# Weight slots as contiguous rows, cast once, and read back in bf16 from a scratch tensor

## The reference

```
h = rmsnorm(x); [u | gb | gc | v] = h @ w_in              # 1024 -> 2048
A = (trailing means of u over 2/4/8/16 tokens - u) @ w_pool * scale
B = gb * causal_conv3(gc * v)
x += [A | B] @ w_out                                      # 1024 -> 1024
h = rmsnorm(x); up = causal_conv3(h @ w_up) + bias        # 1024 -> 2 x 2816
x += (silu(gate) * val) @ w_down                          # 2816 -> 1024
y = rmsnorm(x)                                            # and new pool, conv and ffn states
```

## Time and profile before

| | us |
|---|---|
| median of 3 runs | 893.31 |
| lowest and highest run | 893.15, 897.61 |
| span of the profiled execution (slowest core, core 5) | 899.7 |
| the other cores' spans | 853.4 to 892.1 |
| PE busy | 743.1 (83%) |
| DVE, ACT, POOL busy | 506.7, 360.7, 345.8 |

### The profile page before, as it was taken

The page is one execution under the profiler, slowest core; times in us unless marked ns, Lnnn a source line. Parts: engine busy times, 40 slices in busy tenths (PEclk is TensorE's granted clock), DMA queues, the critical chain, the costliest instruction groups (busy, mean ns, idle before and its releaser), DMA issues.

```text
span 899.7 us, 13434 instructions; the slowest of 8 cores (853.4 to 899.7 us)
## 1 busy us (share of the span) xinstructions
PE 743.1 (83%) x3826; PEld 336.7 (37%) x3826; DVE 506.7 (56%) x878; ACT 360.7 (40%) x846; POOL 345.8 (38%) x501
## 2 busy tenths in 40 slices
PE   1765797698999669977899869988899778988996
PEld 0322353344454324433344324433344334333442
DVE  2463467578744635666654646666643645766832
ACT  3221355466722222554552223554542322645621
POOL 5342037477610320466640320566630320566500
PEclk9979899799999989999999979999999989999999
DMA  8999469999972893599992695699992792899921
GB/s 237 140 133 141 65 63 138 133 108 111 86 94 83 175 139 38 51 115 122 123 108 94 171 154 49 56 122 117 125 98 94 158 143 29 74 112 120 118 83 71
DMA packets 265451, 98.74 MB, mean 110 GB/s; under 512 B 251662, under 2 KB 256142, under 8 KB 265378
## 3 DMA queue, kind: packets, MB, share of 16 engines
q0 software_dynamic: 257280, 70.93, 85.0%
q1 hardware_dynamic: 8098, 26.95, 9.2%
HBM read 158.75 MB, written 10.01 MB: 188 GB/s over the span
## 4 chain that ended last, share of the span: by engine, by line
PE 42%; DMA 36%; DVE 8%; issue 7%; ACT 6%; POOL 1%; SPq 1%; DVEq 0%; ACTq 0%; POOLq 0%
PE G L450 24%; DMA wslot<-w_up 21%; DMA wslot<-w_in 11%; PE G L665 8%; PE G L664 8%; ACT hbuf L391 2%; DMA xrot<-xp 2%; DMA x<-xp 2%; DVE x L672 1%; DVE x L673 1%; PE TR L414 1%; PE G L690 1%; ACT rs_all L393 1%; DVE hbuf L403 1%; ACT hb L391 1%
## 5 line engine op out<-in xcount | busy, mean ns | idle before, releaser
L450 PE MATMUL G<-aT,wslot 128*128 128x512 bf16 x1408 | 324.3, 385 | 36.8 <-DMA wslot<-w_up 29.7
L373 POOL DMA_DIRECT2D wslot<-w_up x176 | 158.6, 903 | 168.5 <-PE G L450 122.2
L450 PEld LDWEIGHTS G<-aT,wslot 128*128 128x128 bf16 x1408 | 133.5, 99 | 218.1 <-issue 76.6
L774 ACT ACTIVATE arena<-G,cst_sb 128x512 f32<-128x512 f32 x176 | 134.8, 777 | 146.1 <-PE G L450 146.0
L783 DVE SCALAR_TENSOR_TENSOR arena<-G,cst_sb,arena 128x512 f32<-128x512 f32 x176 | 130.4, 750 | 101.6 <-ACT Esave L799 71.5
L450 PE MATMUL G<-hT,wslot 128*128 128x512 bf16 x512 | 129.3, 411 | 57.2 <-DMA wslot<-w_in 48.7
L803 POOL TENSOR_TENSOR actT<-arena 128x512 bf16<-128x512 f32 x88 | 95.9, 1090 | 114.1 <-ACT arena L770 76.0
L664 PE MATMUL G<-w_down_sb,actT 128*128 128x512 bf16 x352 | 133.4, 379 | 0.0
L665 PE MATMUL G<-w_down_sb,actT 128*128 128x512 bf16 x352 | 133.4, 379 | 0.0
L792 DVE SCALAR_TENSOR_TENSOR arena<-G,cst_sb,arena 128x512 f32<-128x512 f32 x176 | 125.5, 745 | 5.0 <-DVE OFp L790 0.5
L373 POOL DMA_DIRECT2D wslot<-w_in x64 | 57.5, 902 | 139.5 <-PE G L450 138.4
(11 more groups left out here) (116 smaller groups left out, 612.2 us busy)
## 6 DMA issues: line engine op xcount, KB each, us to landing
wslot<-w_up POOLq DMA_DIRECT2D x176, 256.0 KB, 10.7
wslot<-w_in POOLq DMA_DIRECT2D x64, 256.0 KB, 18.9
x<-xp SPq DMA_DIRECT2D x16, 512.0 KB, 12.2
yp<-x SPq DMA_DIRECT2D x16, 512.0 KB, 2.9
xrot<-xp SPq DMA_DIRECT2D x12, 512.0 KB, 8.1
w_down_sb<-w_down POOLq DMA_DIRECT2D x11, 512.0 KB, 20.5
w_out_sb<-w_out POOLq DMA_DIRECT2D x4, 512.0 KB, 31.1
stf_sb<-st_ffn SPq DMA_DIRECT2D x1, 704.0 KB, 8.0
```

The costliest lines, as they stand in the source:

```text
L373: P.op("pool", lambda e, slot=slot, c0=c0, src=src: e.dma_start(out=wslot[slot][:, :, c0:c0 + 128], in_=src.rearrange("(k p) n -> p k n", ...
L450: ins = e.matmul(out_ap, lhsT=wslot[slot][:, k, half * 128:(half + 1) * 128], rhs=rhsT[:, k, 0:ncols], start=(k == 0), stop=(k == nk - 1))
L774: P.op("act", lambda e, tp=tp, g=g, c=c, h=h: e.activation(out=tp[:, h, 2:514], in_=G[g][:, :], func=AF.Identity, scale=cc(C_FW + 3 * c), ...
```

## The change

The host lays the slots out as one tensor `w_str` of 30 slots, each 128 rows of 2048 floats, in the order of use; the values are those of `w_in` and `w_up`. `w_out`, `w_down` and `w_pool` are laid out with one row per partition too. In pass 1 POOL loads a slot in one DMA, which casts: 128 runs of 8 KB in, 128 runs of 4 KB out. When a slot is about to be used there, SP stores it in bf16 in the internal tensor `w_scr`. In passes 2 to 4 SP loads the slots from `w_scr`, without a cast, and POOL issues no DMA any more.

```
+    w_scr = nc.dram_tensor("w_scr", [NSLOT, 128, 2048], BF16, kind="Internal").ap()
...
-        res_dma(w_pool_sb[:], w_pool.rearrange("(g c) d -> c g d", c=128), "wpool", "D_wpool")
+        res_dma(w_pool_sb[:].rearrange("p a b -> p (a b)"), w_pool[:, :], "wpool", "D_wpool")
         for q in range(4):
-            res_dma(w_out_sb[:, :, q * 256:(q + 1) * 256],
-                    w_out[:, q * 256:(q + 1) * 256].rearrange("(k p) n -> p k n", p=128), ("wout", q), f"D_wout{q}")
+            res_dma(w_out_sb[:, 2 * q:2 * q + 2, :].rearrange("p a b -> p (a b)"),
+                    w_out[:, q * 2 * D:(q + 1) * 2 * D], ("wout", q), f"D_wout{q}")
         for q in range(11):
-            res_dma(w_down_sb[:, 2 * q:2 * q + 2, :],
-                    w_down[q * 256:(q + 1) * 256, :].rearrange("(k p) n -> p k n", p=128), ("wdown", q), f"D_wdown{q}")
+            res_dma(w_down_sb[:, 2 * q:2 * q + 2, :].rearrange("p a b -> p (a b)"),
+                    w_down[:, q * 2 * D:(q + 1) * 2 * D], ("wdown", q), f"D_wdown{q}")
...
+        def load_slot(wi, slot):
+            t = wplan[wi]
+            sl = wslot[slot][:].rearrange("p a b -> p (a b)")
+            if wi < NSLOT:
+                P.op("pool", lambda e: e.dma_start(out=sl, in_=w_str[t, :, :]), writes=[("W", slot)], dsem=f"D_w{slot}")
+                unsaved.append((t, slot, sl))
+            else:
+                P.op("sp", lambda e: e.dma_start(out=sl, in_=w_scr[t, :, :]), reads=[("scr", t)],
+                     writes=[("W", slot)], dsem=f"D_h{slot}")
+
+        unsaved = []
+
+        def save_slot():
+            t, slot, sl = unsaved.pop(0)
+            P.op("sp", lambda e: e.dma_start(out=w_scr[t, :, :], in_=sl), reads=[("W", slot)],
+                 writes=[("scr", t)], dsem=f"D_s{slot}")
+
         def prefetch(upto):
             while wissued[0] <= min(upto, len(wplan) - 1):
                 wi = wissued[0]
                 slot = wi % NW
-                for h, (c0, src) in enumerate(wplan[wi]):
-                    P.op("pool", lambda e, slot=slot, c0=c0, src=src: e.dma_start(
-                        out=wslot[slot][:, :, c0:c0 + 128], in_=src.rearrange("(k p) n -> p k n", p=128)),
-                        writes=[("W", slot, h)], dsem=f"D_w{slot}_{h}")
+                load_slot(wi, slot)
                 wissued[0] += 1
                 if wi >= 1:
                     issue_resident(1)
...
         def next_weights(ahead=0):
             wi = wuse[0]
             wuse[0] += 1
+            if wi < NSLOT:
+                save_slot()
             prefetch(wi + NW - 1 - ahead)
             return wi % NW
```

More of the change, by code:

```diff
@@ L28 @@
 WINDOWS = (2, 4, 8, 16)
+NSLOT = 8 + NFF
+S1_COL = {"u": 0, "gb": 512, "gc": 1024, "v": 1536}
+S1_PAIRS_G = ((("gc", 0), ("v", 0)), (("gb", 0), ("gc", 1)), (("u", 3), ("u", 2)), (("v", 1), ("gb", 1)),
+              (("gc", 2), ("v", 2)), (("u", 1), ("u", 0)), (("gb", 2), ("gc", 3)), (("v", 3), ("gb", 3)))
 NW = 4
@@ L169, in build_nc @@
     xsm = din("xsm", [NSM, D])
[L170 to L174, removed]
+    w_str = din("w_str", [NSLOT, 128, 2048])
+    w_out = din("w_out", [128, 8 * D])
+    w_down = din("w_down", [128, NFF * D])
+    w_pool = din("w_pool", [128, 512])
     cst = din("cst", [128, NCST])
@@ L335, in build_nc @@
         P.op("sp", lambda e: e.dma_start(out=gfin_sb[:], in_=gfin[:, :]), writes=["gfin"], dsem="D_gfin")
[L337 to L346, removed]
+        wplan = [t for _ in range(NST) for t in range(NSLOT)]
         wissued = [0]
@@ L452, in f @@
                 return ins
-            P.op("pe", f, reads=[("W", slot, half)] + rhs_keys, writes=[gk(g), gt(g)])
+            P.op("pe", f, reads=[("W", slot)] + rhs_keys, writes=[gk(g), gt(g)])
         S1_PAIRS = S1_PAIRS_G
@@ L692, in f @@
                 return ins
-            P.op("pe", f, reads=[("wout", 0), ("wout", 1)], writes=[gk(g), gt(g)])
+            P.op("pe", f, reads=[("wout", 0)], writes=[gk(g), gt(g)])
             gdone(g)
@@ L969 @@
     gfin = np.ascontiguousarray(np.broadcast_to(f(norm_final)[None, :], (128, D)))
+    wi0, wu0 = f(w_in)[0].reshape(8, 128, 2048), f(w_up)[0].reshape(8, 128, 2 * DFF)
+    w_str = np.zeros((NSLOT, 128, 8, 256), np.float32)
+    for i, pair in enumerate(S1_PAIRS_G):
+        for h, (kind, j) in enumerate(pair):
+            c0 = S1_COL[kind] + 128 * j
+            w_str[i, :, :, h * 128:(h + 1) * 128] = wi0[:, :, c0:c0 + 128].transpose(1, 0, 2)
+    for j in range(NFF):
+        for h in range(2):
+            c0 = h * DFF + 128 * j
+            w_str[8 + j, :, :, h * 128:(h + 1) * 128] = wu0[:, :, c0:c0 + 128].transpose(1, 0, 2)
+    w_str = w_str.reshape(NSLOT, 128, 2048)
     shared = {
-        "w_in": f(w_in)[0], "w_up": f(w_up)[0], "w_out": f(w_out)[0], "w_down": f(w_down)[0],
-        "w_pool": f(w_pool)[0].reshape(512, 128), "cst": cst, "gfin": gfin,
+        "w_str": w_str,
+        "w_out": np.ascontiguousarray(f(w_out)[0].reshape(8, 128, D).transpose(1, 0, 2)).reshape(128, 8 * D),
+        "w_down": np.ascontiguousarray(f(w_down)[0].reshape(NFF, 128, D).transpose(1, 0, 2)).reshape(128, NFF * D),
+        "w_pool": np.ascontiguousarray(f(w_pool)[0].transpose(1, 0, 2)).reshape(128, 512), "cst": cst, "gfin": gfin,
     }
```

## The result

The changed kernel takes **858.04 us** (median of 5 runs, 847.29 to 858.56), the kernel before 897.61 us beside it (893.15 to 913.33): a ratio of **0.9548, 95% interval 0.9482 to 0.9615**. It is faster by 4.5%, where 10.9% was forecast: 0.9548 x 893.31 is 853 us, where 796 was forecast and 825 was the top of the range. The profiled execution took 847.29 us, with a span of 845.6 us on core 1; against 899.7 us the span fell by 54 us, not by 98. It lies 11 us under the median because in the other four executions two cores of one die had a granted clock of 0.93 to 0.94, and the slowest of them (854 to 857 us) set the time.

What follows compares the result with a forecast made beforehand. Weight DMA in small packets was taken as the bound. Pass 1 gives -14 up to stage 2 and -10 in stage 3, later stages 1 -29, later stages 3 -45: -98, span 801.7, scaled to 796 us; range 770 to 825.

Steps and rivals of the forecast that it cites:

- Stage 3, passes 2 to 4: Later passes' stage 3: 22 iterations of 3.47 us, 76.3 us each, scratch loads hidden; 229.0 against 274.9 us, -45.
- the small packets cost the time, not the bytes: Software queue's weight loads: 275-byte packets hold its engines 85.0% of the span; SP's queue moves 26.95 MB in 9.2%.
- Stage 1, passes 2 to 4: Later passes' stage 1: 3 x 29.4 us plus 15.7 of waits behind x1 reloads, 104 against 132.9 us, -29.
- the base of 29.4 us: Each later stage 1 without waits: eight pairs of 3.47 us and 1.6 us to the first `w_out` matmul.
- the prices here are those of the full clock, since the waits left are shorter: Later stages 1 were priced at full clock, though the granted clock there fell to 0.88 to 0.92 before the change.
- Pass 1 up to stage 2: Start of pass 1: DMA stays the bound, slot 7 lands at 71 us, stage 2 begins at 85; -14.
- I take the middle, 27: Pass 1's last x tile lands between 18 and 36 us; taken as 27, so stage 1 starts at 37.
- Seven pairs of 5.05 us: Stage 1 of pass 1: from a start at 37 us the pairs end at 72, one us after slot 7's landing.
- Stage 3 of pass 1: Pass 1's stage 3: between 114 us (all engine work) and 93 (PE's floor), 107 taken against 116.8; -10.
- Pass 1 gains nothing: Rival for pass 1: slower cast packets, saves beside every load, late x; 812 to 830 us, chance 0.18.
- The slower case: Rival for later passes: scratch loads as a closed loop of four slots; at 15 us a load about 910, chance 0.02.
- Cores closer together than 46 us: Sign of a right forecast: the cores' ends lie closer together than the 46 us before the change.

## Why the prediction was wrong where it was

The span fell by 54 us, not by 98. Of the 44 missing, pass 1 up to stage 2 has 13.8, stage 3 of pass 1 15.6, the later stages 1 12.9 and the rest, forecast at nothing, 3.6; the later stages 3 gave 2 more than forecast.

- **Stage 3, passes 2 to 4: right.** -47.0 for -45, at 76.0 us each, and the scratch loads land in 3.4 us. (3 x 76.3 against 274.9 is -46, not -45.) But the sentence "the small packets cost the time, not the bytes" holds only with eight cores running: alone, the same packets cost PE nothing here. And the forecast credited the whole change with it, where either half does nearly all of it.
- **Stage 1, passes 2 to 4: mechanism right, size off.** The waits of 8.03, 3.78 and 5.41 us answer to 7.7, 4 and 4. The term that failed is the base of 29.4 us. The sentence "the prices here are those of the full clock, since the waits left are shorter" was wrong: behind a wait of 3.78 us the granted clock was 0.80, and 0.73 at the pass's start, after the 2.19 us that PE waited there. And the undisturbed floor is 31.7 (pass 2 of the layout with six buffers, pass 3 with late reloads), in which PE also waits for DVE (1.5 us ahead of the last pairs). 3 x 31.7 and the waits' 17.2 are 112.3; the slower matmuls beside the waits account for the rest to 116.8.
- **Pass 1 up to stage 2: wrong, -0.2 for -14.** Two steps failed. The start is the smaller part, 41.4 us for 37. "I take the middle, 27": the last x tile landed at 35.8 us, which is the end of the range named beside it, "36 us, all casts first". The rows had both ends and no reason for the middle. In the changed kernel's first 36 us the software queue holds 50.2% of the engines and SP's 45.6%, and with x first the start came at 29.0. The larger part is the way from the start to stage 2, 57.0 us for 48. "Here DMA stays the bound" and "Seven pairs of 5.05 us" were wrong: PE waits for no weights there, but 15.3 us for ACT and DVE, among them 6.78 and 4.09 us in one piece, and the stage takes 57.1 us on one core and 56.5 on one core with the old layout, where the longest wait is the same one (7.03 us). The chain of DVE and ACT work had no term. The rule of the Trainium skill (DMA: Bandwidth & Descriptors, Queues, rings and completion order) that an engine takes its rows in turn, packet by packet, gave -5 by the working of that place, nearer than -14. The delay of x is what it says; that -5 came near is luck besides, since it had stage 1 start at 46 us and last 48.
- **Stage 3 of pass 1: wrong in sign, +5.6 for -10.** Of the two ends, 114 "that counts all the work" and 93, I took 107. The measured shares say that all the work does count: 84 us of casts and 32 of SP's queue, 116 where I had 106, and with the 8 us of tail and latency on top 124, near the 122.4. No run shows an overlap of loads and saves that saves time: without the saves the stage is 13 to 16 us shorter. Mis-sized besides: a slot's cast. 12.42 MB written in 84 us are 3.55 us for each 0.52 MB, not the 3.07 taken from the 2 KB packets of the earlier trace rows; on one core they are 69 us of a stage of 109. PE's floor of 93 was not within reach either: with six buffers and no saves the stage takes 100, and 99.6 us is the shortest of any run. That the number of buffers counts too had no term: with six of them and all the saves the stage takes 101.8 us.
- **The rivals.** "Pass 1 gains nothing" (812 to 830, 0.18) was the case that came, as its reasons "saves to HBM join every load, and x lands late" said; its price had no stage 3 longer than before and no lower clock, so the 853 us lie above its 830 too. The slower case wanted a scratch load to take 13.3 us: it took 3.4. The packets did become long.
- **Cores closer together than 46 us: right**, 12.7. With the layout alone it is 13.9 us, with the old layout and six buffers 28.7, so most of the spread comes with the small packets.
- **How the range was made.** The three terms that failed had two ends each, and I took a value inside every time. All three came out past the dear end (-16 for -20, -0.2 for -5, 122 for 114), and the range, cut at one case in ten on each side, did not allow for that.

## What to carry to other kernels

When a change adds traffic to engines that are near full, add all engine times of the stage up, each queue's share by its length, and take the sum as the forecast; overlap inside an engine needs a row that shows it. Before a cache in a scratch tensor is built, try the cheap half (here long rows) alone and look at what is left: here the second half gave 4 us in stage 3 and took 29 elsewhere, 14 of them by the place of four DMA issues. Try spare buffers before either: two idle tiles gave as much as the whole change. A price that was read with all cores running belongs to all cores, and one run on one core tells it apart from the core's own.
